# Two prompt steps of a head pair made one, and gate products in units of 512 and 256 tokens, in a one-core diffusion layer

## The chip, the cores and the metric

The kernel runs on one NeuronCore of a Trainium2 chip. Its engines run side by side and meet at semaphores: TensorE (PE, matmuls and transposes), VectorE (DVE), ScalarE (ACT), GpSimd (POOL), and SyncE (SP), which issues most DMAs. The metric is device time in microseconds (us); lower is better.

## The reference

One transformer layer serves 1024 latent tokens and 256 prompt tokens with the same weights. `D_IN` holds queries, keys and values of two attention branches, a gate `z` for each, and two merge gates.

```python
h = _rmsnorm(x) * (1.0 + scale) + shift
qa, ka, va, za, qb, kb, vb, zb, ga, gb = split(h @ w_in)
oa = attention_a(qa, ka, va)      # 8 heads; latent: 2-D neighbourhood + 512 cached keys, one softmax
ob = attention_b(qb, kb, vb)      # 8 heads on 2 kv heads, rotary, +-128 window + 512 cached keys + a sink logit
ya = (oa * silu(za)) @ w_br_a
yb = (ob * silu(zb)) @ w_br_b
y  = rmsnorm(x + gate * ((sigmoid(ga) * ya + sigmoid(gb) * yb) @ w_out))
```

Prompt tokens see only the 256 prompt tokens (branch b adds the sink logit there too). All is float32 in and out; each product is made of three passes of split operands.

## The kernel before

`front` makes the normalised, split input `h` ("hm") and the values. `pairs` then runs a loop over four pairs of heads for branch a and again for branch b (the last pair of b is written out apart), and `finish` does the two branch projections, the merge and the output.

A pair begins with projections (`project`: 6 for branch a, 3 for branch b, a third of them 256 tokens wide, the rest 512), each handled by ACT and DVE (`projected`; in branch b with the rotary arithmetic on DVE). Then come `STEPS` = 10 attention steps. Steps 0 and 1 are the prompt of head 0 and of head 1; steps 2 to 9 are blocks of latent queries (sample steps). Each step has 2 columns of softmax statistics (`t`). A step is a chain over four engines:

- PE `scores(s)` into PSUM `s_ps`; DVE `minima(s)` (scores are negated, so the maximum is a minimum; sample steps in branch a first add a bias that POOL prepares in `comb`); ACT `exps(s)`; DVE `normalise(s)`;
- PE `transposes(s, c)` in chunks `c` (two of four blocks, then one of four and one of two; a prompt step has one chunk) into two banks `t_ps`; ACT `high` and DVE `low` copy each chunk out in two parts;
- PE `weighted(s, 0)` and `weighted(s, 1)` (values times probabilities; a prompt step has only the first); ACT `low_half`, DVE `add_halves`.

The order on each engine is written by hand. On PE, step `s` is: `scores(s)`, `weighted(s-2, 1)`, the first two chunks of `transposes(s-1)`, `unit(s)`, the remaining chunks of `transposes(s-1)`, `weighted(s-1, 0)`. A `unit` is a piece of the gate products (3 blocks of 1280 tokens a pair, 24 matmuls per piece into the one PSUM bank `d_ps`). It is what PE does while the softmax chain of the step runs on DVE and ACT. There are 12 units of 320 tokens: one in each step, then `unit(10)` and `unit(11)` in the tail. ACT copies a unit to `gst` (two slots, a tile of its own) and stores it to DRAM (`gate`, `gate_out`).

In branch b, `scores(0)` stands ahead of the last projection (`EARLY` = 2) and the rest of the prompt chain is woven into it. In branch a it stands behind all projections.

SP loads in order: the caches of a pair into `craw` (after the previous pair's caches are split), a weight tile, the values `vw` and `vp`, bias blocks for `comb`, more weight tiles. Tiles are split on ACT and DVE (`tile_high`, `tile_low`) at the steps that the table `SPLITS` names.

Of the kernel before, what the change touches and what calls it, by code (L numbers as in the profile page):

```python
# [41 lines left out]
P = 128  # L42
# [25 lines left out]
UNIT = 320  # L68
UNITS = TOK // UNIT
# [3 lines left out]
STEPS = 10  # L73
CHUNKS = [1, 1] + [4] * 8
# [565 lines left out]
def pairs(nc, io, block, hm, ident, wt, wraw, craw, w_in, w_hi, w_lo, tiles, own, counts, earlier_stage, branch, f=None):  # L640
# [12 lines left out]
    q1, q2, kk, kc, pr, pt, ost, gst, otmp = (tiles[n] for n in ("q1", "q2", "kk", "kc", "pr", "pt", "ost", "gst", "otmp"))  # L653
# [8 lines left out]
    if A:  # L662
        comb, rowm, colm = (own[n] for n in ("comb", "rowm", "colm"))
        kout = otmp
# [12 lines left out]
    LAST_AT = 8  # L677
# [6 lines left out]
    EARLY = None if A else 2  # L684
    PROMPT_READY = 4 if A else 1
    COMB_FREE = [0, 0, 6, 10, 12, 14]
# [57 lines left out]
    def chunk_blocks(s):  # L744

        if s < 2:
            return [[(0, 0), (0, 1), (1, 0), (1, 1)]]
# [15 lines left out]
    def _(sp):  # L763
# [6 lines left out]
        def body(p, last):  # L770
# [16 lines left out]
            def load_caches():  # L787
                sp.wait_ge(c_split, pb * 3)
# [21 lines left out]
            sp.wait_ge(pvb_done, pb * (STEPS - 2))  # L810
# [62 lines left out]
    def _(pe):  # L873
        def body(p, last):
# [17 lines left out]
            def unit(u):  # L892

                i, t0 = PROJ + u // UNITS, (u % UNITS) * UNIT
                if u % UNITS == 0:
# [3 lines left out]
                pe.wait_ge(g_done, pb * GPP * UNITS + u)  # L899
                mm = split_mm(pe, d_ps[:, 0:UNIT], lambda a, k: tile(i, a, k),  # L900
                              lambda b, k: hm[:, b, k, t0:t0 + UNIT], KD)
                mm.then_inc(d_done, 1)

            def score(s, t, out, rhs):

                if s < 2:
                    h, cols = s, lambda ap: ap[..., LAT + t * P:LAT + (t + 1) * P]
                elif A:
                    h, cols = (s - 2) // 4, lambda ap: ap[..., (4 * t + (s - 2) % 4) * P:(4 * t + (s - 2) % 4 + 1) * P]
                else:  # L910
                    h, cols = t, lambda ap: ap[..., (s - 2) * P:(s - 1) * P]
# [3 lines left out]
            def scores(s):  # L915
# [6 lines left out]
                else:  # L922
                    if s == 2:
# [3 lines left out]
                for t in range(2):  # L927
                    if s < 2:
                        mm = score(s, t, s_ps[:, 2 * t, 0:PROMPT], lambda h, r: kk[r, h, LAT:TOK])
# [1041 lines left out]
```

## Time and profile before

| | us |
|---|---|
| median of 3 runs | 1283.93 (1282.22 to 1284.35) |
| the profiled execution's own time | 1281.49 |
| its span, first to last instruction | 1279.7 |
| PE busy | 1224.1 (96%) |
| DVE / ACT busy | 833.5 (65%) / 617.8 (48%) |
| granted TensorE clock | 0.993 of full speed |

A busy PE is not PE at its peak: ends of matmuls are modelled and overlap, so the length of a piece of work is read from its start to the start of the next.

### The profile page before, as it was taken

How to read it: one execution, taken by the hardware profiler on the slowest of the kernel's cores; microseconds unless marked ns; L12 is line 12 of the kernel's file. 1: busy time of each engine (PE TensorE's matmuls, PEld its weight loads, DVE VectorE, ACT ScalarE, POOL GpSimd, SP SyncE). 2: the span in 40 equal slices, each digit the busy share in tenths (PEclk: the TensorE clock that was granted, in tenths of full speed). 3: DMA queues.
4: the chain of work that ended last, by engine and by line, in shares of the span. 5: the costliest groups of instructions: out<-in, count | busy, mean ns of one | idle time of the engine just before them, and what ended most of it. 6: DMA issues, size and time to landing. Idle time of an engine off the chain costs nothing. (4 is left out here: it accounts for less than half of the span.)

```text
span 1279.7 us, 23385 instructions
## 1 busy us (share of the span) xinstructions
PE 1224.1 (96%) x7888; PEld 1111.7 (87%) x7888; DVE 833.5 (65%) x1674; ACT 617.8 (48%) x1239; POOL 194.7 (15%) x203
## 2 busy tenths in 40 slices
PE   6999999999999999999999989999999989899997
PEld 1599889988998899899889989989988988898996
DVE  2469458757755875687688588588678875444342
ACT  3432335534643554355466456546546664543441
POOL 0000023104300520231000000000000024433440
PEclk9999999999999999999999999999999999899999
DMA  9356532133214213321511411421221557444440
GB/s 360 134 182 193 195 115 75 55 122 118 74 59 139 79 62 110 123 67 52 181 55 38 132 48 37 116 65 37 74 90 39 189 170 241 149 148 148 159 154 33
DMA packets 87257, 147.67 MB, mean 115 GB/s; under 512 B 7558, under 2 KB 65542, under 8 KB 87180
## 3 DMA queue, kind: packets, MB, share of 16 engines
q1 hardware_dynamic: 70476, 124.64, 30.3%
q10 hardware_dynamic: 16704, 22.15, 4.8%
q8 instruction: 30, 0.49, 0.2%
q14 instruction: 47, 0.39, 0.1%
HBM read 111.37 MB, written 35.40 MB: 115 GB/s over the span
## 5 line engine op out<-in xcount | busy, mean ns | idle before, releaser
L83 PE MATMUL d_ps_pairs<-h,wt 128*128 128x320 f32 x2304 | 359.3, 311 | 0.0
L83 PEld LDWEIGHTS d_ps_pairs<-h,wt 128*128 128x128 f32 x2304 | 338.8, 188 | 0.3
L1087 ACT ACTIVATE pr<-s_ps_pairs,mx 128x896 f32<-128x896 f32 (+1 forms) x160 | 143.1, 897 | 84.4 <-DVE mx L1315 44.0
L1272 DVE TENSOR_TENSOR pt<-t_ps_pairs,pt 128x512 fp32r<-128x512 f32 (+1 forms) x272 | 158.3, 621 | 37.1 <-ACT pt L1076 35.8
L83 PE MATMUL s_ps_pairs<-h,wt 128*128 128x512 f32 (+1 forms) x864 | 167.6, 354 | 0.0
L83 PEld LDWEIGHTS s_ps_pairs<-h,wt 128*128 128x128 f32 x864 | 141.9, 189 | 21.9
L1076 ACT ACTIVATE pt<-t_ps_pairs 128x512 fp32r<-128x512 f32 (+1 forms) x272 | 135.1, 547 | 34.7 <-PE t_ps_pairs L949 29.1
L949 PE MATMUL t_ps_pairs<-ident_sb,pr 128*128 128x128 f32 x960 | 133.0, 276 | 13.0 <-DVE pt L1272 6.1
L949 PEld LDWEIGHTS t_ps_pairs<-ident_sb,pr 128*128 128x128 f32 x960 | 108.3, 140 | 23.2 <-DVE pt L1272 12.8
L1699 PE MATMUL y_ps<-wo,mg 128*128 128x512 f32 x480 | 113.2, 396 | 0.0
L1663 POOL TENSOR_TENSOR tp<-tp 128x256 f32<-128x256 f32 x40 | 31.3, 783 | 517.5 <-DVE tp L1751 516.2
L1699 PEld LDWEIGHTS y_ps<-wo,mg 128*128 128x128 f32 x480 | 90.0, 188 | 21.6
L864 POOL TENSOR_TENSOR comb_a<-rowm_a,comb_a 128x384 f32<-128x384 f32 x48 | 51.4, 1071 | 324.5 <-DMA comb_a<-in_bias 324.5
L1284 DVE TENSOR_REDUCE mn<-s_ps_pairs 128x2 f32<-128x1024 f32 (+1 forms) x72 | 83.6, 1162 | 23.9 <-PE s_ps_pairs L913 22.7
L1331 DVE TENSOR_SCALAR pr<-pr,rden 128x896 f32<-128x896 f32 (+1 forms) x160 | 96.2, 644 | 2.8
L83 PE MATMUL b_ps<-og,wb 128*128 128x256 f32 x720 | 90.0, 287 | 5.4 <-DVE tp L1751 5.4
L83 PEld LDWEIGHTS b_ps<-og,wb 128*128 128x128 f32 x720 | 89.0, 193 | 6.1 <-DVE tp L1751 4.0
L1136 ACT ACTIVATE otmp<-o_ps_pairs 64x256 f32<-64x256 f32 x80 | 30.5, 382 | 114.1 <-PE o_ps_pairs L977 113.3
L1104 ACT ACTIVATE gst<-d_ps_pairs 128x320 f32<-128x320 f32 x96 | 41.8, 435 | 79.5 <-PE d_ps_pairs L83 79.5
L83 PE MATMUL v_ps<-wv,h 128*128 128x320 f32 x480 | 73.1, 311 | 0.0
L83 PEld LDWEIGHTS v_ps<-wv,h 128*128 128x128 f32 x480 | 70.7, 188 | 1.0 <-issue 0.9
L1751 DVE TENSOR_TENSOR tp<-b_ps,gt 128x256 f32<-128x256 f32 x80 | 32.5, 422 | 44.1 <-PE b_ps L83 42.5
(168 smaller groups left out, 1687.4 us busy)
## 6 DMA issues: line engine op xcount, KB each, us to landing
gates_d<-gst ACTq DMA_DIRECT2D x96, 160.0 KB, 1.8
wraw<-in_w_gate SPq DMA_DIRECT2D x24, 512.0 KB, 3.5
gt<-gates_d SPq DMA_DIRECT2D x40, 256.0 KB, 4.0
comb_a<-in_bias SPq DMA_DIRECT2D x24, 384.0 KB, 3.4
vw_a<-v_d SPq DMA_DIRECT2D x64, 128.0 KB
v_d<-vst SPq DMA_DIRECT2D x20, 320.0 KB, 4.5
wada<-in_w_ada SPq DMA_DIRECT2D x12, 512.0 KB, 5.7
kk<-kb_d SPq DMA_DIRECT2D x16, 320.0 KB, 5.8
```

Of the source, the lines that this page charges most:

```text
L83: mm = eng.matmul(out, lhs(a, k), rhs(b, k), start=(k == 0 and i == 0), stop=(k == n_k - 1 and i == 2))
L864: pool.tensor_tensor(c, rm, c, ALU.subtract).then_inc(comb_t, 1)
L949: mm = pe.transpose(t_ps[:, n % 2, b * P:(b + 1) * P], probs_block(s, t, kb), ident[:, :])
L1076: act.activation(pt[:, 0, c * 512:c * 512 + cols], t_ps[:, n % 2, 0:cols], ACT.Copy).then_inc(hi_done, 1)
L1087: act.activation(probs_run(s, t), scores_run(s, t), ACT.Exp, bias=mx[:, t:t + 1], scale=-1.0, accum_out=den[:, t:t + 1]).then_inc(exp_done, 1)
L1104: act.activation(gst[:, u % 2, :], d_ps[:, 0:UNIT], ACT.Copy).then_inc(g_done, 1)
L1272: dve.tensor_tensor(pt[:, 1, c * 512:c * 512 + cols], t_ps[:, n % 2, 0:cols], pt[:, 0, c * 512:c * 512 + cols].bitcast(F32), ALU.subtract) ...
L1284: red = dve.tensor_reduce(ctx_min[:, :], s_ps[:, :, :].rearrange("p (t b) c -> p t b c", b=2)[:, :, s % 2 if s >= 2 else 0, 0:width], AX.X ...
L1331: dve.tensor_scalar(probs_run(s, t), probs_run(s, t), rden[:, t:t + 1], None, ALU.mult).then_inc(p_done, 1)
L1663: pool.tensor_tensor(tp[:, j % 2, 0, :], tp[:, j % 2, 0, :], tp[:, j % 2, 1, :], ALU.add).then_inc(summed, 1)
L1699: mm = pe.matmul(y_ps[:, e, n * 512:(n + 1) * 512], mg[:, a, k, e * P:(e + 1) * P], wo[k][:, b, n * 512:(n + 1) * 512], start=(k == 0 and ...
L1751: dve.tensor_tensor(tp[:, j % 2, br, :], b_ps[:, j % 2, br, 0:CT], gt[(j + 2) % GSLOTS][:, br, :], ALU.mult).then_inc(b_prod, 1)
```

## The change

Steps 0 and 1 become one step 0 with four columns (two heads by two blocks of queries), so `STEPS` = 9 and the sample steps are 1 to 8. Its scores fill four halves of two PSUM banks, its maxima, sums and reciprocals are four wide, and its eight transposed blocks are two full chunks. In branch a `scores(0)` and the maxima now also stand ahead of the last projection (`EARLY` = 5). In both branches all of `normalise(0)` comes behind it. The 12 units become 10, of 512 or 256 tokens, so there is one unit a step and one in the tail (`unit(9)`). The copies of the units go to `craw`, the buffer that the caches are loaded into, so the next pair's cache loads wait until all gate stores of this pair have landed, and the first copy of a pair waits until the caches are split. In `finish` the raw weights rotate over the staging buffers in another order, and the load into `craw` stands behind the last gate store.

```diff
-UNIT = 320
-UNITS = TOK // UNIT
+UNITS = [(0, 0, 512), (0, 512, 512), (0, 1024, 256), (1, 0, 512), (1, 512, 512), (1, 1024, 256),
+         (2, 0, 256), (2, 256, 256), (2, 512, 512), (2, 1024, 256)]
+NU = len(UNITS)
-STEPS = 10
-CHUNKS = [1, 1] + [4] * 8
+STEPS = 9
+SAMPLES = STEPS - 1
+CHUNKS = [2] + [4] * SAMPLES
...
+    gst = craw[:, :].rearrange("p (u c) -> p u c", u=2)
-        SPLITS = [(3, 0, 1), (4, 0, 2), (2, 1, 6), (0, 1, 9), (1, 1, STEPS)]
+        SPLITS = [(3, 0, 1), (4, 0, 2), (2, 1, 4), (0, 1, 7), (1, 1, STEPS)]
-        SPLITS = [(2, 0, 1), (0, 1, 2), (3, 0, 5), (1, 1, STEPS)]
+        SPLITS = [(2, 0, 1), (0, 1, 2), (3, 0, 4), (1, 1, STEPS)]
-    EARLY = None if A else 2
+    EARLY = 5 if A else 2
...
             def load_caches():
-                sp.wait_ge(c_split, pb * 3)
+                for slot in range(2):
+                    sp.wait_ge(g_out[slot], pb * (NU // 2) * 16)
...
             def scores(s):
-                    if s == 2:
+                    if s == 1:
                         pe.wait_ge(x_used, p * NG + NG)
                         pe.wait_ge(c_split, pb * 3 + 3)
...
-                    if s < 2:
-                        mm = score(s, t, s_ps[:, 2 * t, 0:PROMPT], lambda h, r: kk[r, h, LAT:TOK])
+                    if s == 0:
+                        for head in range(2):
+                            mm = score(s, t, prompt_scores(t, head), lambda h, r: kk[r, h, LAT:TOK], head)
                         continue
...
-                if 4 <= s < STEPS:
+                if 3 <= s < STEPS:
                     weighted(s - 2, 1)
...
-            unit(STEPS + 1)
             weighted(STEPS - 1, 1)
...
             def gate(u):
-                act.wait_ge(g_out[u % 2], (pb * (GPP * UNITS // 2) + u // 2) * 16)
-                act.activation(gst[:, u % 2, :], d_ps[:, 0:UNIT], ACT.Copy).then_inc(g_done, 1)
+                if u == 0:
+                    act.wait_ge(c_split, pb * 3 + 3)
+                act.wait_ge(g_out[u % 2], (pb * (NU // 2) + u // 2) * 16)
+                act.activation(gst[:, u % 2, 0:n], d_ps[:, 0:n], ACT.Copy).then_inc(g_done, 1)
...
-            gate(STEPS + 1)
-            gate_out(STEPS + 1)
+            gate_out(STEPS)
...
+            def prompt_minima():
+
+                dve.wait_ge(s_done, pb * STEPS + 1)
+                both = s_ps[:, :, :].rearrange("p (t b) (h c) -> p t b h c", b=2, h=2)[:, :, 0, :, :]
+                grid4 = lambda ap: ap[:, :].rearrange("p (t h) -> p t h", h=2)
                 if A:
+                    dve.tensor_reduce(grid4(mx), both, AX.X, ALU.min).then_inc(m_done, 2)
                     return
...
-                    if n == EARLY:
-                        normalise(0)
...
                 if n == EARLY:
-                    minima(0)
+                    prompt_minima()
                 projected(n)
+            normalise(0)
...
-        sp.wait_ge(c_split, 3 * ALL)
+        sp.wait_ge(s_done, ALL * STEPS)
         load_w(2)
-        sp.wait_ge(s_done, ALL * STEPS)
         load_w(3)
+        sp.wait_ge(w_lo, TILES_TOTAL)
         load_w(4)
...
+        sp.wait_ge(g_out[0], ALL * HALF * 16)
+        sp.wait_ge(g_out[1], ALL * HALF * 16)
+        load_w(5)
...
-        own_f.update(wb=wb, wo=wo, stage=[craw[:, :], x[:, 0, :], x[:, 1, :], wraw[:, :]])
+        own_f.update(wb=wb, wo=wo, stage=[x[:, 0, :], x[:, 1, :], wraw[:, :], craw[:, :]])
```

PE at the prompt of a branch a pair, before, from the last projection to the first sample scores (`h,wt` into `s_ps` is a projection, into `d_ps` a unit, `kk,q` are scores over own keys, `kc,q` over cached keys, `vp_a` the prompt's weighted sum):

```order
L83 MATMUL s_ps_pairs<-h,wt 128x512 x24
L912 MATMUL s_ps_pairs<-kk,q 128x256
...
L83 MATMUL d_ps_pairs<-h,wt 128x320 x24
...
L912 MATMUL s_ps_pairs<-kk,q 128x256
...
L949 MATMUL t_ps_pairs<-ident_sb,pr 128x128 x4
...
L83 MATMUL d_ps_pairs<-h,wt 128x320 x24
...
L977 MATMUL o_ps_pairs<-pt,vp_a 128x256 x4
...
L912 MATMUL s_ps_pairs<-kc,q 128x512
```

The same place of the change:

```order
L928 MATMUL s_ps_pairs<-kk,q 128x256
L929 MATMUL s_ps_pairs<-kk,q 128x256
...
L86 MATMUL s_ps_pairs<-h,wt 128x512 x24
...
L86 MATMUL d_ps_pairs<-h,wt 128x512 x24
...
L928 MATMUL s_ps_pairs<-kc,q 128x512
...
L966 MATMUL t_ps_pairs<-ident_sb,pr 128x128 x8
...
L86 MATMUL d_ps_pairs<-h,wt 128x512 x24
...
L995 MATMUL o_ps_pairs<-pt,vp_a 128x256 x8
```

All prompt scores moved ahead of the last projection. The first sample scores (`kc,q`) stand behind one unit of 512, where two units of 320 and two sets of prompt scores stood.

PE in the tail of a branch a pair, before:

```order
L83 MATMUL d_ps_pairs<-h,wt 128x320 x24
...
L949 MATMUL t_ps_pairs<-ident_sb,pr 128x128 x2
...
L977 MATMUL o_ps_pairs<-pt,vc_a 128x256 x8
...
L83 MATMUL d_ps_pairs<-h,wt 128x320 x24
...
L977 MATMUL o_ps_pairs<-pt,vw_a 128x128 x2
L977 MATMUL o_ps_pairs<-pt,vw_a 128x256 x4
L977 MATMUL o_ps_pairs<-pt,vw_a 128x128 x2
```

The tail of the change:

```order
L86 MATMUL d_ps_pairs<-h,wt 128x256 x24
...
L966 MATMUL t_ps_pairs<-ident_sb,pr 128x128 x2
L978 REGISTER_ALU
L995 MATMUL o_ps_pairs<-pt,vc_a 128x256 x8
L976 REGISTER_ALU
L995 MATMUL o_ps_pairs<-pt,vw_a 128x128 x2
L995 MATMUL o_ps_pairs<-pt,vw_a 128x256 x4
L995 MATMUL o_ps_pairs<-pt,vw_a 128x128 x2
```

The unit between the last two weighted sums (`vc_a`, then `vw_a`) is gone, so nothing stands between them now.

## Rows read from the trace of the kernel before

**Rows 1.** Busy time by stretch: one pair of branch a, one of branch b

```profile
core 0: us, PE busy (x) PEld busy (x) DVE busy (x) ACT busy (x) POOL busy (x), PEclk, DMA share, GB/s
380.60:497.60 117.00, 114.79 (x763) 107.35 (x762) 79.86 (x154) 56.83 (x114) 25.26 (x24) 1.00 0.28 91
720.00:825.00 105.00, 100.45 (x676) 94.06 (x675) 78.72 (x182) 57.91 (x133) 0.00 (x0) 1.00 0.23 68
```

**Rows 2.** Timeline of PE, a steady step: start, us, engine, line, operation [wait]

```profile
441.05 0.82 PE L949 MATMUL t_ps_pairs<-ident_sb,pr 128*128 128x128 f32 x6
...
442.65 0.39 PE L912 MATMUL s_ps_pairs<-kc,q 128*128 128x512 f32 x1
...
444.29 1.03 PE L977 MATMUL o_ps_pairs<-pt,vw_a 128*128 128x128 f32 x8
...
445.97 3.76 PE L83 MATMUL d_ps_pairs<-h,wt 128*128 128x320 f32 x24
449.58 0.82 PE L949 MATMUL t_ps_pairs<-ident_sb,pr 128*128 128x128 f32 x6
```

**Rows 3.** Timeline of PE, branch a, prompt scores to fourth step

```profile
408.24 0.28 PE L912 MATMUL s_ps_pairs<-kk,q 128*128 128x256 f32 x1
...
424.55 0.73 PE L977 MATMUL o_ps_pairs<-pt,vp_a 128*128 128x256 f32 x4 [0.83 <-DVE pt L1272]
...
434.00 0.40 PE L912 MATMUL s_ps_pairs<-kc,q 128*128 128x512 f32 x1
```

**Rows 4.** Timeline of PE, tail of that pair to the next pair's first projection

```profile
488.84 1.03 PE L949 MATMUL t_ps_pairs<-ident_sb,pr 128*128 128x128 f32 x8
...
497.64 2.73 PE L83 MATMUL s_ps_pairs<-h,wt 128*128 128x512 f32 x11
```

**Rows 5.** Timeline of PE, branch b, first unit to the transposes of step 3

```profile
734.35 3.68 PE L83 MATMUL d_ps_pairs<-h,wt 128*128 128x320 f32 x24
...
764.34 1.03 PE L949 MATMUL t_ps_pairs<-ident_sb,pr 128*128 128x128 f32 x8
```

**Rows 6.** Timeline of PE, a projection of 512 tokens in branch b

```profile
728.88 5.63 PE L83 MATMUL s_ps_pairs<-h,wt 128*128 128x512 f32 x24
```

**Rows 7.** Chain that ended last: start us, us, what (192 matmuls of 256 columns)

```profile
1135.49 23.04 PE b_ps L83 x192
```

**Rows 8.** Timeline of DVE, branch a, step 3: first reduction, then low copies

```profile
428.26 1.22 DVE L1284 TENSOR_REDUCE mn<-s_ps_pairs 128x2 f32<-128x1024 f32 x1
...
431.43 1.29 DVE L1272 TENSOR_TENSOR pt<-t_ps_pairs,pt 128x512 fp32r<-128x512 f32 x2
```

**Rows 9.** Page, part 5: the exponentials (mean of one)

```profile
L1087 ACT ACTIVATE pr<-s_ps_pairs,mx 128x896 f32<-128x896 f32 (+1 forms) x160 | 143.1, 897 | 84.4 <-DVE mx L1315 44.0
```

**Rows 10.** Timeline of DVE, branch b: prompt minima, last queries of the last projection

```profile
734.99 0.69 DVE L1284 TENSOR_REDUCE mn<-s_ps_pairs 128x2 f32<-128x512 f32 x1
...
741.15 1.39 DVE L1263 TENSOR_TENSOR q<-rot_b,q 64x512 fp32r<-64x512 f32 x2
```

**Rows 11.** Timeline of DVE, branch b, a steady step: first reduction, last low copies

```profile
772.18 1.23 DVE L1284 TENSOR_REDUCE mn<-s_ps_pairs 128x2 f32<-128x1024 f32 x1 [0.85 <-PE s_ps_pairs L913]
...
779.11 1.01 DVE L1272 TENSOR_TENSOR pt<-t_ps_pairs,pt 128x512 fp32r<-128x512 f32 x2
```

**Rows 12.** Timeline of SP, branch a, the pair's first tile load

```profile
384.76 0.33 SPq L785 DMA_DIRECT2D wraw<-in_w_gate  x1
```

**Rows 13.** Timeline of POOL, last operation on the pair's first bias block: pair 1, pair 3

```profile
185.02 1.88 POOL L866 TENSOR_TENSOR comb_a<-comb_a,colm_a 128x384 f32<-128x384 f32 x1
...
418.80 1.02 POOL L866 TENSOR_TENSOR comb_a<-comb_a,colm_a 128x384 f32<-128x384 f32 x1
```

**Rows 14.** Page, part 6: DMA issues of the gate stores, the last figure us to landing

```profile
gates_d<-gst ACTq DMA_DIRECT2D x96, 160.0 KB, 1.8
```

**Rows 15.** Source line 789, the cache key loads: time to landing

```profile
DMA to landing us min/median/max: 3.8/5.1/9.0
```

**Rows 16.** Timeline of PE, tail of the last pair and the first branch products

```profile
1025.80 1.03 PE L949 MATMUL t_ps_pairs<-ident_sb,pr 128*128 128x128 f32 x8
...
1037.12 4.58 PE L83 MATMUL b_ps<-og,wt 128*128 128x256 f32 x36 [1.28 <-DVE og L1452]
```

More of the change, by code:

```diff
@@ L744, in chunk_blocks @@
     def chunk_blocks(s):
-        if s < 2:
-            return [[(0, 0), (0, 1), (1, 0), (1, 1)]]
+        if s == 0 and A:
+            return [[(2 * h + kb, t) for kb in range(2) for t in range(2)] for h in range(2)]
+        if s == 0:
+            return [[(2 * h + kb, t) for h in range(2) for t in range(2)] for kb in range(2)]
         if A:
@@ L977, in weighted @@
                         mm = pe.matmul(o_ps[:, c0 * P:(c0 + nb) * P], v, pt[:, part, b0 * P:(b0 + nb) * P],
-                                       start=(half == 0 and n == 0 and part == 0),
-                                       stop=((half == 1 or s < 2) and n == len(work) - 1 and part == 1),
+                                       start=(half == 0 and part == 0 and (n == 0 or (s == 0 and c0 > 0 and n == 2))),
+                                       stop=(part == 1 and ((half == 1 and n == len(work) - 1)
+                                                            or (s == 0 and n % 2 == 1))),
                                        skip_group_check=True)
@@ L989, in body @@
             for s in range(STEPS + 1):
-                if s < STEPS and not (s == 0 and EARLY):
+                if 0 < s < STEPS:
                     scores(s)
-                if 4 <= s < STEPS:
+                if 3 <= s < STEPS:
                     weighted(s - 2, 1)
@@ L1086, in exps @@
                         act.wait_ge(r_done, pb * STEPS + s)
+                    if s == 0:
+                        for h in range(2):
+                            c = 2 * t + h
+                            ex = act.activation(prompt_probs(t, h), prompt_scores(t, h), ACT.Exp, bias=mx[:, c:c + 1],
+                                                scale=-1.0, accum_out=den[:, c:c + 1])
+                            if h == 1:
+                                ex.then_inc(exp_done, 1)
+                            if not A:
+                                es = act.activation(esk[:, c:c + 1], nsk[:, h:h + 1], ACT.Exp, bias=mx[:, c:c + 1],
+                                                    scale=-1.0)
+                                if h == 1:
+                                    es.then_inc(esk_done, 1)
+                        continue
                     act.activation(probs_run(s, t), scores_run(s, t), ACT.Exp, bias=mx[:, t:t + 1], scale=-1.0,
@@ L1140, in body @@
                     split_caches()
+                if A and n == EARLY:
+                    exps(0)
                 projected(n)
@@ L1151, in body @@
                     high(s - 1, range(min(2, CHUNKS[s - 1])))
-                if s < STEPS and not (s == 0 and EARLY):
+                if 0 < s < STEPS:
                     exps(s)
+                if s < STEPS:
                     gate(s)
@@ L1160, in body @@
                     tile_highs(s)
-                if last and s == 6:
-                    act.wait_ge(o_done, pb * STEPS + 4)
+                if last and s == 5:
+                    act.wait_ge(o_done, pb * STEPS + 3)
                     act.dma_start(io["o_d"][pb, :, 0:2 * P], ost[:, 0:2 * P]).then_inc(o_out, 16)
@@ new lines, in minima @@
+                if not A:
+                    dve.wait_ge(band_in, 16)
+                for t in range(2):
+                    near = comb[:, n % 2, t, :] if A else band[:, 0 if s == 1 else 2 if s == STEPS - 1 else 1, :]
+                    bank = near_bank(s, t)
+                    red = dve.tensor_tensor_reduce(bank, bank, near, 1.0, BIG, ALU.add, ALU.min, nm[:, t:t + 1])
+                red.then_inc(m2_done, 1)
+                dve.wait_ge(m1_done, p * SAMPLES + s if A else p * STEPS + s + 1)
@@ L1383, in body @@
                         first_gated(dve, f, 0)
-                if s < STEPS and not (s == 0 and EARLY):
+                if 0 < s < STEPS:
                     normalise(s)
```

194 lines of the change are left out of this document (94 added, 100 removed).

## The prediction

> **What bounds the kernel.** I read the busy time by stretch first. In one pair of branch a PE is busy 114.8 of 117.0 us, in one of branch b 100.5 of 105.0, at a granted clock of 1.00 [rows 1]; DVE, the next engine, has 79 us of work in either. So PE sets the pace, and there are two things to gain: the price of PE's own work, and the places where PE waits. The timeline of PE says where those are. A steady step of branch a has a period of 8.53 us: 1.60 for six transposes and the cached part of the weighted sum, 1.64 for scores, 1.68 for the near part and eight transposes (0.1 each), 3.61 for the unit, with no wait [rows 2]. The waits stand at both ends of a pair.
>
> Branch a, from the prompt scores to the scores of step 4, takes 25.76 us [rows 3]. The work in it is 0.96 of prompt scores (8 of 256 columns at 0.120 [rows 7]), 3.52 + 3 x 3.61 of units, 1.5 of transposes, 1.60, 3.28 of sample scores, 0.96 of prompt weighted sums: 22.65. So 3.1 us are lost; the longest single wait is 0.83, for DVE's low copies [rows 3]. The tail takes 8.80 us [rows 4] for 1.68 + 1.60 + 3.52 + 0.87 = 7.67 of work: 1.1 lost. In branch b, the 29.99 us from unit(0) to the transposes of step 3 [rows 5] hold 14.35 of units, 0.48 + 4.92 of scores, 3.1 of transposes and cached sum, 0.96 and 0.72 of weighted sums, 24.5 in all: 5.5 lost. A prompt step has little PE work of its own, and its chain is longer than one unit.
>
> **The change part by part, per pair.**
>
> *Units.* 320 tokens cost 24 x 147 ns = 3.52 us. 512 tokens with the same operand `h` cost 734.35 - 728.88 = 5.47 [rows 5, 6], 256 cost 24 x 0.120 = 2.88 [rows 7]. Twelve units are 42.24, five of each new size 41.75, and one change-over of 0.09 (3.61 against 3.52) goes: 0.6 us gained. That is about 11 ns a matmul beyond the columns, and 48 matmuls fewer.
>
> [...]
>
> *Step 1 (first sample step).* In branch a, `scores(0)` is followed by a projection and unit(0), 5.47 us each, so the prompt chain is covered. The next scores end 0.96 + 5.47 + 1.64 = 8.1 us after the projections, at 416.3 on the old scale. The old place of the first sample scores' end was 419.6. DVE first wants the bias block there, and POOL has it at 418.80 + 1.02 = 419.8 [rows 13]: 3.5 us late. But SP's work comes earlier. Its first tile load stood 4.1 us after the pair's start [rows 12, 1], because `tile_high` stood behind the copy and store of unit(11). Now the last unit ends some 5 us before the pair does, and the tile is split about 1.7 us sooner; the value loads and bias loads behind it on SP follow. So DVE is 1.8 late. Cover: from the scores' end PE has 0.8 of transposes, 5.47 of unit(1), 0.96 of weighted sum, 7.2 in all. The chain is 1.8 + 2.5 (minima: DVE's first copy stands 3.17 after its first reduction [rows 8], of which 2.5 is the minima) + 2 x 0.9 and read-outs of exponentials, some 2.1 [rows 9]: 6.4. Hidden, with 0.8 to spare. In the first pair the block comes at 186.9 [rows 13] in a pair begun at 145.7, 5.5 after it is wanted, with no tail ahead of it: PE waits 2.9 for the low copies and some 0.5 in the next step.
>
> *Step 2* has a unit of 256, and two `add_halves` ahead of the low copies. DVE begins 0.35 late (tile split of step 1), the low copies end 431.43 + 1.29 - 428.26 = 4.45 later [rows 8], plus 0.4 for the second addition. PE wants the first of two banks at 0.8 + 2.9 = 3.7 and gets it at about 4.5, the second later still: 1.0 us lost. This is the new place of the old wait.
>
> *Steps 5 to 7* also have 256. PE's period falls to 8.53 - 0.64 = 7.9 in branch a, 7.7 in b. DVE's chain in b is 779.11 + 1.01 - 772.18 = 7.94 from the scores to the last low copy [rows 11]; PE wants this at 7.7. I take 0.2 a step, 0.6. Branch a has no sink arithmetic and I take 0.
>
> *Branch b, step 1.* The sample scores need all queries, so they wait for the rotary work of the last projection. The old minima began at 734.99, the last query was done at 741.15 + 1.39 = 742.5 [rows 10], with 1.05 of `normalise(0)` in between, which now comes after. The minima are 0.45 longer. That makes 742.0. Unit(0) now ends at 734.35 + 0.48 + 5.47 = 740.3: PE waits 1.75. What is late next, `normalise(0)` (1.6 us), then lies beside the scores (1.64).
>
> *Tail.* The 1.1 lost there stays. unit(11) hid the last low copies; without it the near sum follows the cached sum (1.03) at once and waits 0.3.
>
> *craw.* The last gate store is issued some 3.9 us after the last unit and takes 1.8 to land [rows 14]; the caches follow, 5.1 at the median [rows 15], and are in 5.9 us into the next pair. ACT reaches them at 5.1 in branch b, where DVE takes them at 7.3 behind the first queries; 0.6 for ACT's first copy leaves about 1 us. Cost 0; this cover is thin.
>
> *Sums.* Branch a: before 3.1 + 1.1 = 4.2 lost. After: 0.2 (restarts) + 1.0 + 1.1 + 0.4 = 2.7. With 0.6 of units: 2.1 a pair, 6.3 for three; the first pair gives 2.1 + 1.1 (its own old wait was that much longer) - 3.4 = -0.2. Branch b: 6.6 before; after 1.85 + 1.0 + 0.2 + 0.6 + 1.4 = 5.05; with 0.6, 2.15 a pair, 6.5 for three. The last pair differs: from the end of its second last unit to 1037.12 takes 11.3 us, and the last wait is for DVE's `first_gated` chain [rows 16], which starts from the transposes and not from unit(11). Dropping unit(11) there saves nothing, while its tokens are done earlier: 41.75 - 11 x 3.52 = +3.0, less 2.2 of waits saved: 0.8 slower. In `finish` the new order of loads puts each ahead of its use, since its chain hangs on DVE and on stores of `o_d` after the same point: 0.
>
> Total -0.2 + 6.3 + 6.5 - 0.8 = 11.8, say 12 us, from the profiled span 1279.7 and the 1.8 around it: 1269.5. That execution was 2.4 below the median of the runs shown, so the median goes from 1283.9 to **1272**.
>
> **The rivals.**
>
> *Larger gain, 0.10.* DVE's order in step 2 leaves no wait, because the chunks arrive as in the old steady step, and the projection and unit prices hold. 8 x 1.0 more: 1264. Against it: 4.45 of chain on a cover of 3.7.
>
> *Bias late, 0.10.* SP's loads do not come sooner, since cache loads now stand in front of the tile. The chain in step 1 is then 8.1 against 7.2 and drags step 2: 1.4 for each of three pairs, 1276.
>
> *Short units expose the chain, 0.10, no change.* Each 256 step gives back the 0.64 by which its unit is shorter, wherever it stands: four steps a pair, 2.6 instead of the 1.0 to 1.6 taken, and the copies of 512 columns on ACT delay the transposes' copies by some 0.2 a step. 1.5 a pair, twelve in all: 1284. For it: DVE's 7.94 in branch b. Against: DVE waits 0.85 in that step [rows 11].
>
> *Caches late, slower, 0.10.* The loads wait for a store's landing and were early before. Branch b has four pairs with 1 us of slack; every further us comes off unit(0)'s cover and lengthens the wait at the first sample scores. The decisive point is a landing 3 to 4 us later than I take it, near the 9.0 maximum [rows 15]: beyond 10.5 us into the pair the 12 us are gone. At 12 us: 1288.
>
> [...]
>
> **How the numbers follow.** A measurement of this kernel tells about 0.2% (2.6 us) from no change. My forecast has 0.60 with its own range 1267 to 1277, from 1 us either way for step 2 over half the pairs, 0.5 for the wait of branch b at the first sample scores, and 0 to 0.5 for the tail. With the larger gain and the late bias that is 0.80 of faster, 0.10 of same and 0.10 of slower. The range for 8 in 10 reaches to both of the faster rivals: 1263 to 1280.
>
> **What would show it.** In the changed profile: unit steps of 5.5 and 2.9 us; a wait of PE on DVE's low copies behind the unit of step 2, near 1 us; in branch b a wait ahead of the first `kc,q` scores of 1.5 to 2; no wait ahead of the prompt's weighted sum, except in the first pair (about 3); pairs of about 115 and 103 us, the last about 105. It would be wrong if the cache loads land later than 7 us into a pair, if POOL's first block delays every pair, or if a step with 256 takes longer than 8 us.

## The result, and the profile after

The changed kernel takes 1297.2 us (median of 4 runs, 1294.6 to 1298.4) against 1284.1 for the kernel before: a ratio of 1.010, with a 95% interval of 1.008 to 1.012. It is 1% slower. The forecast was 1272, range 1263 to 1280; it missed in sign. The profiled execution has a span of 1296.6 us against 1279.7.

I read the busy time by stretch first, with one stretch for each pair (boundaries are PE's first projection of a pair; the last pair's ends at the first product of `finish`). The row behind the dots is a stretch of `finish`. The columns are those of [rows 1].

```profile
145.62:265.93 120.31, 115.77 (x715) 103.12 (x713) 79.76 (x152) 57.08 (x113) 25.25 (x26) 0.99 0.28 90
265.93:381.87 115.94, 113.95 (x714) 102.03 (x714) 79.21 (x152) 56.04 (x111) 22.96 (x24) 1.00 0.29 92
381.87:498.07 116.20, 114.20 (x714) 102.00 (x714) 79.87 (x152) 55.81 (x111) 22.95 (x24) 1.00 0.28 91
498.07:616.92 118.85, 115.16 (x715) 103.47 (x714) 78.85 (x152) 55.82 (x111) 23.06 (x25) 0.99 0.35 109
616.92:723.49 106.57, 100.55 (x622) 89.53 (x622) 78.16 (x178) 57.41 (x129) 0.00 (x0) 0.98 0.24 75
723.49:832.70 109.21, 101.85 (x623) 90.67 (x622) 78.22 (x178) 57.21 (x129) 0.00 (x0) 0.97 0.22 66
832.70:941.75 109.05, 102.27 (x622) 91.03 (x621) 78.23 (x178) 57.22 (x129) 0.00 (x0) 0.97 0.21 66
941.75:1048.36 106.61, 100.58 (x622) 88.34 (x621) 82.65 (x186) 62.53 (x137) 0.00 (x0) 0.99 0.30 101
...
1051.85:1152.29 100.44, 95.16 (x565) 85.58 (x566) 54.54 (x83) 47.38 (x71) 41.96 (x40) 0.94 0.57 186
```

Against the same points of the kernel before (118.0, 116.9, 117.0, 117.7 in branch a, 104.8, 104.8, 104.7, 107.5 in branch b; for the last pair up to the second group of products in `finish`, 1037.12 [rows 16] and now 1051.85), the pairs are longer by 2.3, -1.0, -0.8, 1.2, 1.8, 4.4, 4.3 and 2.6 us, and what follows by 2.2: the 17 us of the two spans. Two pairs of branch a go as forecast in kind. Most of what the forecast missed lies at the ends of pairs ahead of branch b, at the start of branch b's pairs, and in the granted clock, which is now 0.97 to 0.99 in six pairs instead of 1.00. The waits of PE and of ACT, summed, name the two places:

```profile
PE t_ps_pairs L966 <- DVE pt L1304: 18.3, 17, 2.8
...
PE s_ps_pairs L928 <- DVE q L1295: 8.8, 4, 3.2
```

```profile
ACT craw L1135 <- DMA gates_d<-craw: 19.0, 4, 5.0
```

(total us, times, longest.) Before, PE's first row stood at 6.1 us in 13 times, and its trace had neither of the other two.

**The tail.** Timelines of ACT, then of SyncE, then of PE, at the end of the first pair of branch b:

```profile
711.67 0.34 ACTq L1127 DMA_DIRECT2D gates_d<-craw  x1
...
717.69 0.38 ACT L1135 ACTIVATE craw<-d_ps_pairs 128x256 f32<-128x256 f32 x1 [4.64 <-DMA gates_d<-craw]
...
718.36 1.08 ACT L1093 ACTIVATE pt<-t_ps_pairs 128x512 fp32r<-128x512 f32 x2 [0.28 <-ACT craw L1135]
```

```profile
708.97 2.76 SPq L822 DMA_DIRECT2D kk<-kb_d  x4
```

```profile
716.23 0.96 PE L995 MATMUL o_ps_pairs<-pt,vw_b 128*128 128x256 f32 x6
719.73 1.54 PE L966 MATMUL t_ps_pairs<-ident_sb,pr 128*128 128x128 f32 x6 [2.54 <-DVE pt L1304]
720.92 2.02 PE L995 MATMUL o_ps_pairs<-pt,vc_b 128*128 128x256 f32 x8
```

The copy of the last unit, `gate(9)`, needs slot 1 of the raw buffer, which unit 7's store must have left. That store is issued only inside `gate(8)`, at 711.67. SyncE had begun four key loads of 320 KB at 708.97, and the store lands 5.9 us after its issue, where the median before was 1.8 [rows 14]. ACT stands for 4.64 us. Some 2.6 of them it would have stood anyway, since PE ends the unit near 715.6; so the store had 3.9 us and came 2.0 late. The high copies are behind it, DVE's low copies behind those, and PE's transposes wait 2.54. This happens at the four pair ends ahead of a pair of branch b (2.3 to 2.8 us) and at no other. Before, the store that the copy at 711.67 needed went out just ahead of the key loads, landed in 1.8 us and had 5.05. The one that the last copy needed, at 711.82, was behind those loads too and took 4.5 us, but unit(11) left it 7.75; ACT's rows of that kernel, then SyncE's:

```profile
706.62 0.34 ACTq L1098 DMA_DIRECT2D gates_d<-gst  x1
...
711.67 0.44 ACT L1104 ACTIVATE gst<-d_ps_pairs 128x320 f32<-128x320 f32 x1 [3.67 <-PE d_ps_pairs L83]
711.82 0.34 ACTq L1098 DMA_DIRECT2D gates_d<-gst  x1
...
719.57 0.44 ACT L1104 ACTIVATE gst<-d_ps_pairs 128x320 f32<-128x320 f32 x1 [4.29 <-PE d_ps_pairs L83]
```

```profile
706.69 2.47 SPq L807 DMA_DIRECT2D kk<-kb_d  x4
```

**The clock.** Busy time by stretch at that tail and at the next pair's first sample scores; the column behind the engines is the granted clock:

```profile
716.00:718.00 2.00, 1.19 (x11) 0.98 (x9) 0.00 (x0) 0.31 (x1) 0.00 (x0) 1.00 0.33 76
718.00:720.00 2.00, 0.27 (x2) 0.27 (x2) 1.01 (x2) 1.54 (x4) 0.00 (x0) 0.84 0.35 131
720.00:722.00 2.00, 2.00 (x11) 2.00 (x11) 1.23 (x4) 0.91 (x3) 0.00 (x0) 0.50 0.00 0
722.00:724.00 2.00, 2.00 (x16) 2.00 (x16) 0.53 (x2) 1.33 (x2) 0.00 (x0) 0.81 0.72 281
744.00:746.00 2.00, 0.00 (x0) 0.00 (x0) 1.49 (x4) 1.78 (x4) 0.00 (x0) 1.00 0.00 0
746.00:748.00 2.00, 1.00 (x2) 0.83 (x3) 1.89 (x7) 0.00 (x0) 0.00 (x0) 0.67 0.00 0
748.00:750.00 2.00, 2.00 (x7) 1.79 (x6) 0.36 (x2) 0.00 (x0) 0.00 (x0) 0.50 0.00 0
```

At both places PE has stood for 2.5 to 3.2 us, and then runs at 0.50; the rows come to 3.4 us of it at each. The eight scores from 747.00 take 3.12 us, up to 750.12, instead of 1.73 at full clock (experiment 6).

**The start of branch b's pairs.** Timeline of ACT in the second pair of branch b, and PE's wait there:

```profile
724.84 0.34 ACTq L1216 DMA_DIRECT2D o_d<-ost  x1
728.36 0.38 ACT L1071 ACTIVATE rot_b<-s_ps_pairs 128x256 f32<-128x256 f32 x1 [4.29 <-issue]
...
733.11 0.42 ACT L1049 ACTIVATE vc_b<-craw 128x256 fp32r<-128x256 f32 x1 [2.15 <-issue]
```

```profile
747.00 0.79 PE L928 MATMUL s_ps_pairs<-kc,q 128*128 128x512 f32 x1 [3.15 <-DVE q L1295]
```

The forecast had 1.75 for this wait. It is 1.85 in the first pair and 1.42 in the last, but 3.15 and 2.38 in the two pairs that ACT enters by the loop's jump back. There ACT is idle for nothing the profile shows ("issue"), once ahead of its first copy and once, five activations on, ahead of the value cache's. Before, ACT copied 0.87 us behind its last store's issue, and had no such idle. Queue q14, of the kind that the page calls "instruction", moved six blocks of 8 KB in the 20 us from 720, against three before (whose they were, the profile doesn't say):

```profile
q14 instruction: 6, 0.05, 0.8%
```

### The profile page after: what moved, and what is told of

Its sections match the earlier page's. It is cut to its first block and busy times, and to the rows that moved or that the text cites. A ratio compares the mean times of both kernels' runs of the same rounds, so it can differ in the third digit from the quotient of the medians.

```text
span 1296.6 us, 22309 instructions
## 1 busy us (share of the span) xinstructions
PE 1231.4 (95%) x7488; PEld 1080.5 (83%) x7488; DVE 830.4 (64%) x1650; ACT 610.9 (47%) x1215; POOL 186.0 (14%) x203
## 5 line engine op out<-in xcount | busy, mean ns | idle before, releaser
L86 PE MATMUL d_ps_pairs<-h,wt 128*128 128x512 f32 (+1 forms) x1920 | 351.9, 339 | 0.0
L86 PEld LDWEIGHTS d_ps_pairs<-h,wt 128*128 128x128 f32 x1920 | 295.2, 189 | 36.0
L1117 ACT ACTIVATE pr<-s_ps_pairs,mx 128x896 f32<-128x896 f32 x128 | 128.1, 1004 | 64.7 <-DVE mx L1326 36.7
L1314 DVE TENSOR_REDUCE mn<-s_ps_pairs 128x2 f32<-128x1024 f32 x64 | 78.0, 1219 | 41.7 <-POOL comb_a L881 24.3
L879 POOL TENSOR_TENSOR comb_a<-rowm_a,comb_a 128x384 f32<-128x384 f32 x48 | 43.5, 905 | 334.9 <-DMA comb_a<-in_bias 334.9
L1368 DVE TENSOR_SCALAR pr<-pr,rden 128x896 f32<-128x896 f32 x128 | 87.1, 722 | 2.2
L1135 ACT ACTIVATE craw<-d_ps_pairs 128x512 f32<-128x512 f32 (+1 forms) x80 | 39.0, 488 | 96.9 <-PE d_ps_pairs L86 77.7
L1168 ACT ACTIVATE otmp<-o_ps_pairs 64x256 f32<-64x256 f32 (+1 forms) x72 | 29.1, 404 | 117.2 <-PE o_ps_pairs L995 116.8
```

The costliest lines, as they stand in the source:

```text
L86: mm = eng.matmul(out, lhs(a, k), rhs(b, k), start=(k == 0 and i == 0), stop=(k == n_k - 1 and i == 2))
L879: pool.tensor_tensor(c, rm, c, ALU.subtract).then_inc(comb_t, 1)
L1117: act.activation(probs_run(s, t), scores_run(s, t), ACT.Exp, bias=mx[:, t:t + 1], scale=-1.0, accum_out=den[:, t:t + 1]).then_inc(exp_done, 1)
L1135: act.activation(gst[:, u % 2, 0:n], d_ps[:, 0:n], ACT.Copy).then_inc(g_done, 1)
L1314: dve.tensor_reduce(mn[:, 0:2], s_ps[:, :, :].rearrange("p (t b) c -> p t b c", b=2)[:, :, s % 2, :], AX.X, ALU.min).then_inc(m1_done, 1)
L1368: dve.tensor_scalar(probs_run(s, t), probs_run(s, t), rden[:, t:t + 1], None, ALU.mult).then_inc(p_done, 1)
```

## Experiments

Ratios are to the kernel before, measured on the same chip with the kernels beside it, each with its 95% interval; times are medians. "Changed" is 1.0101, from the runs of the result; it was not measured again beside the experiments.

**1. `e1_store7_early`: the store of unit 7 issued at the end of step 7.**

```diff
-                if u > 0:
+                if u > 0 and u != NU - 2:
                     gate_out(u - 1)
...
                     tile_highs(s)
+                if s == NU - 3:
+                    gate_out(s)
```

> The changed kernel with one edit: ACT issues the store of unit 7 at the end of step 7 instead of inside the gate copy of unit 8, which came 2.7 us behind the start of the key loads. Theory T (the last unit waits for the slot of unit 7, whose store stands behind the key loads): the wait of 4.6 us of ACT before the last unit's copy goes, the waits of 2.3 to 2.8 us on PE at the four tails ahead of B pairs fall under 0.6, and with them the half clock of the next 3 to 4 us; four times (2.0 + 1.3 to 2.0), so 13 to 16 us sooner than the changed kernel: about 1283, level with before. Rival C (late caches through the raw buffer are the cost): PE's waits at the tails only move to the next pair's first scores, and the time stays within 4 us of 1297. Rival U (the merged step and the units themselves): 8 us sooner at most, 1289.

1286.1 us, 1.0027 (1.0014 to 1.0041): 9.5 us off. Timeline of ACT at the same tail; no wait for a store is left in the whole trace:

```profile
714.13 0.38 ACT L1135 ACTIVATE craw<-d_ps_pairs 128x256 f32<-128x256 f32 x1 [3.04 <-PE d_ps_pairs L86]
```

PE waits 0.48 there instead of 2.54. The gain is less than expected, because PE's waits for the queries in the next two pairs grew to 4.00 and 3.83.

**2. `e2_kk_after_store`: the key loads wait for unit 7's store.**

```diff
                 sp.wait_ge(exp_done, pb * 2 * STEPS)
+                sp.wait_ge(g_out[1], pb * (NU // 2) * 16 - 16)
                 for h in range(2):
```

(The same wait stands ahead of the cos and sin loads.)

> The changed kernel with one edit: SyncE issues the key loads of B (and the cos and sin loads ahead of the first) only when the store of unit 7 has landed. The store is issued where it was. Theory T says it is the traffic ahead of the store that makes it late: the store then lands 2 us after its issue, ACT's wait ahead of the last copy falls from 4.6 to under 1 us, PE's waits at the tails to about 0.3 as in the A pairs, and the time is 1283 to 1286, if the key loads (5 us later, needed some 18 us later) stay hidden. If it is the late issue and not the traffic, ACT's wait stays over 2.5 us and the time over 1291. Rival C expects the caches not sooner and 1297.

1286.5 us, 1.0027 (1.0011 to 1.0043). The store is issued as late as in the changed kernel, but the copy that needs its slot no longer waits for it:

```profile
708.71 0.34 ACTq L1129 DMA_DIRECT2D gates_d<-craw  x1
...
712.69 0.38 ACT L1137 ACTIVATE craw<-d_ps_pairs 128x256 f32<-128x256 f32 x1 [2.59 <-PE d_ps_pairs L86]
```

Either edit alone removes the same wait: it takes both the late issue and the loads ahead of it. The cost here is that the first pair's caches come later: ACT waits 4.19 us for them, and PE 3.76 for the queries.

**3. `e3_caches_early`: the key cache waits for slot 0 alone, the value cache of branch b goes to free columns.**

```diff
-                for slot in range(2):
-                    sp.wait_ge(g_out[slot], pb * (NU // 2) * 16)
+                sp.wait_ge(g_out[0], pb * (NU // 2) * 16)
                 sp.dma_start(craw[:, 0:PAST], io["ck" + branch][p]).then_inc(craw_in, 16)
+                if A:
+                    sp.wait_ge(g_out[1], pb * (NU // 2) * 16)
+                else:
+                    sp.wait_ge(g_out[1], pb * (NU // 2) * 16 - 48)
-                sp.dma_start(craw[:, PAST:PAST + 4 * CH * HD], io["cv" + branch][p]).then_inc(craw_in, 16)
+                sp.dma_start(craw[:, V0:V0 + 4 * CH * HD], io["cv" + branch][p]).then_inc(craw_in, 16)
```

> The changed kernel with one edit: the key cache is loaded when unit 8's store has landed (its half of the raw buffer), and in B the value cache goes to columns that the last three odd units do not use, so both loads of B are issued about 4 us sooner, before the pair ends. Rival C (late caches): PE's wait ahead of the first cache scores in B (1.9, 3.2, 2.4, 1.4 us) falls by 1 us or more in each pair, and the time by 5 to 8 us to about 1290. Theory T: the query chain on DVE ends that wait, not the caches; the wait falls by 0.5 at most a pair and the time stays at 1294 to 1298.

1294.1 us, 1.0086 (1.0061 to 1.0110), not told apart from 1.0101. The loads of branch b now stand at 719.12 and 719.85, 3.9 us ahead of the pair's start at 723.0, and PE's waits for the queries are 1.85, 2.33, 3.24 and 1.43, in sum what they were. Late caches are not the cause in the changed kernel, where they had landed 2.6 to 4.1 us into each pair of branch b. ACT's two idle stretches are still there, with the caches long in:

```profile
724.30 0.34 ACTq L1220 DMA_DIRECT2D o_d<-ost  x1
727.49 0.39 ACT L1075 ACTIVATE rot_b<-s_ps_pairs 128x256 f32<-128x256 f32 x1 [3.96 <-issue]
...
731.73 0.42 ACT L1053 ACTIVATE vc_b<-craw 128x256 fp32r<-128x256 f32 x1 [1.65 <-issue]
```

**4. `e4_merge_320`: the merged prompt step with twelve units of 320.**

```diff
-UNITS = [(0, 0, 512), (0, 512, 512), (0, 1024, 256), (1, 0, 512), (1, 512, 512), (1, 1024, 256),
-         (2, 0, 256), (2, 256, 256), (2, 512, 512), (2, 1024, 256)]
+UNITS = [(b, t0, 320) for b in range(3) for t0 in range(0, TOK, 320)]
...
                 else:
                     weighted(s - 2, 1)
+                    unit(STEPS + 1)
...
+            unit(STEPS + 2)
             weighted(STEPS - 1, 1)
```

(ACT's copies of the two extra units follow in the same order.)

> The merged prompt step alone: the changed kernel with its units put back to twelve of 320 tokens (nine in the steps, three in the tail), still stored through the raw buffer. Rival U (uneven units and a tail with one unit are the cost): the pairs lose the 1.0 us of step 2 and the DVE waits, but pay the unit price of 0.6 a pair, and the time is 1284 or less, near before. Theory T: the tail copies have three slots to wait for instead of one and the store of unit 7 is still issued behind the key loads, so ACT's wait at the tail stays 3 to 5 us, though part of it lies beside the tail's units: 1288 to 1297.

1306.6 us, 1.0181 (1.0154 to 1.0208), beyond what either theory had, and ACT waits for a store only once (3.9 us) and not at each tail, as Theory T had it. PE's waits, summed:

```profile
PE o_ps_pairs L994 <- DVE pt L1307: 22.7, 16, 5.8
PE s_ps_pairs L927 <- DVE q L1298: 17.7, 4, 5.2
```

The prompt's chain and the queries' chain have 3.52 us of unit for cover where 512 tokens give 5.47: in branch a PE now waits 2.8 to 5.8 us ahead of the prompt's weighted sum, and in branch b 3.8 to 5.2 for the queries. So the wide first units are not a cost but what makes the merged step bearable. The arrangement of three units at the tail is mine, and part of the 9 us may be its. ACT's two idle stretches are absent here: the code has changed, and its loop lies elsewhere.

**5. `e5_act_written_out`: experiment 1, with ACT's loop over the first three pairs of branch b written out.**

```diff
-        with eng.Fori(0, PAIRS if A else PAIRS - 1) as p:
-            body(p, False)
+        if written_out:
+            for p in range(PAIRS - 1):
+                body(p, False)
...
-        turns(act, body)
+        turns(act, body, not A)
```

> The kernel with the store of unit 7 early, and ACT's loop over the first three B pairs written out in the code, with no jump back. Its trace had ACT idle on nothing the profile shows (issue) for 4.3 us at the start of B pairs 2 and 3 and again 2.9 to 3.1 us ahead of the value cache's copy, while the instruction queue moved five blocks there against three in the kernel before; PE's wait for the queries was 4.0 and 3.8 us in those pairs, 2.1 in the first, 1.4 in the last. Theory I (fetching ACT's instructions at the jump back makes the chain late): those waits fall to 1.4 to 2.1, and the two pairs shrink by 2 us each and about 1 more for the clock: 1286 becomes 1280 to 1282. Rival Q (the chain on DVE alone is too long for the cover): the waits stay at 3 us or more and the time within 2 us of 1286.

1278.0 us, 0.9962 (0.9948 to 0.9977): 8 us off experiment 1, and 0.4% faster than the kernel before. The second and third pair of branch b fall from 108.5 and 108.7 to 102.9 each, and their waits for the queries to 1.78 and 1.77. Both idle stretches are gone. In the first pair the value cache lands late (7.2 us behind its issue); ACT waits 3.55 for it, and PE 2.95 for the queries.

**6. `e6_filler`: experiment 1, with eight matmuls ahead of the first sample scores in branch b.** Their product is thrown away.

```diff
+                if s == 1 and not A:
+                    for k in range(8):
+                        pe.matmul(t_ps[:, 0, :], tile(2, 0, k % KD), hm[:, 0, k % KD, 0:512], start=True, stop=True)
```

> The kernel with the store of unit 7 early, and in B eight matmuls of 512 columns ahead of the first scores of step 1, whose product (in the transposes' bank) is thrown away: 1.9 us of added work that lies in the wait for the queries of 2.1, 4.0, 3.8 and 1.4 us. Theory K (what the wait costs beyond its length is the half clock behind it): the granted clock stays at 1 after step 1 in the first and last pair, the scores there take 1.64 us instead of 3.1, and the time falls by 1.3 to 2 us in each pair whose wait gets short, 3 to 6 in all: 1280 to 1283. Rival: the clock falls whatever PE does there, and the filler only adds up to 0.5 us in the last pair: 1286 to 1288.

1281.0 us, 0.9985 (0.9968 to 1.0001): 5 us off experiment 1, though 1.9 us of work was added in each of four pairs; what it fills are waits of 2.12, 4.00, 3.83 and 1.42 us. The first pair of branch b, timeline of PE in experiment 1 and then here:

```profile
636.11 0.77 PE L928 MATMUL s_ps_pairs<-kc,q 128*128 128x512 f32 x1 [2.12 <-DVE q L1297]
...
639.24 1.21 PE L966 MATMUL t_ps_pairs<-ident_sb,pr 128*128 128x128 f32 x8
```

```profile
631.65 1.97 PE L1011 MATMUL t_ps_pairs<-h,wt 128*128 128x512 f32 x8
633.68 0.49 PE L928 MATMUL s_ps_pairs<-kc,q 128*128 128x512 f32 x1
...
635.41 1.04 PE L966 MATMUL t_ps_pairs<-ident_sb,pr 128*128 128x128 f32 x8
```

The same scores take 3.13 and 1.73 us. From 600 to 1080 us no 2 us stretch with a clock under 0.90 is left, where experiment 1 has sixteen. Even the pairs whose wait is only shortened (2.0 and 1.5 us left) stay at full clock. Six of the sixteen lie behind the last tail, where the clock fell in some kernels and not in others; that part is not the filler's doing as far as is shown.

**7. `e7_combined`: experiments 1 and 3, with ACT's and DVE's loops written out.** No new diff.

> The store of unit 7 early, the caches early (the edit that moved nothing on its own), and ACT's and DVE's loops over the first three B pairs written out. If instruction fetch is what made the caches' earlier load worthless, all of it together gives PE waits of 1.4 to 2.0 at step 1 of every B pair and 1278 to 1281, faster than both kernels. If not, the same as with ACT's loop written out alone.

1274.7 us, 0.9942 (0.9920 to 0.9965). Every middle pair is now alike; one of branch a and two of branch b, by stretch:

```profile
494.80:610.50 115.70, 113.96 (x715) 102.02 (x714) 79.23 (x152) 55.89 (x111) 22.81 (x25) 1.00 0.37 112
610.50:713.90 103.40, 99.90 (x624) 88.29 (x622) 78.05 (x178) 56.98 (x129) 0.00 (x0) 1.00 0.25 76
713.90:817.20 103.30, 99.79 (x622) 88.22 (x621) 78.03 (x178) 56.84 (x129) 0.00 (x0) 1.00 0.21 66
```

**8. `e8_before_written_out`: the kernel before, with the same two loops written out.**

> The kernel before the change with ACT's and DVE's loops over the first three B pairs written out; a control for the two runs in which that made the changed kernel 8 us and 12 us faster. Theory I says that the jump back cost the changed kernel and hardly the kernel before: its trace has no idle of ACT there that is put down to issue, ACT starts 0.9 us behind its last store, and three blocks on the instruction queue, so 0 to 1 us a pair for DVE's 1.5 us restart, 1281 to 1284. Rival: any kernel of this form gains 4 to 8 us by it, 1275 to 1279, and then the gain found belongs to the loop and not to what the change did to it.

1281.2 us, 0.9991 (0.9979 to 1.0004). No change that can be told: what writing the loops out gains is a cost that the change brought.

**9. `e9_after_written_out`: the changed kernel, with the two loops written out and the store as it was.**

> The changed kernel with ACT's and DVE's loops over the first three B pairs written out and nothing else; the store of unit 7 stays late. If the two causes add, it is as much slower than the combined kernel (1275) as the changed kernel is over the one with the early store (10 to 11 us): 1285 to 1287. If the tail wait had only hidden the other, it stays at 1290 or more; if the late store mattered only because ACT came late out of the jump, it falls to 1280 or less.

1287.1 us, 1.0037 (1.0019 to 1.0056), as adding the two causes gives. ACT's wait before the last copy is 4.8 to 5.5 us again, and PE's 2.54 at the end of branch a and 2.65, 2.31 and 1.96 at the first three tails in branch b.

**10. `e10_no_early_caches`: experiment 7 without the early caches.**

> The combined kernel without its early cache loads: store of unit 7 early, ACT's and DVE's loops written out. Rival C in its last form (late caches bind once the fetches are out of the way) expects PE's wait at step 1 of B pairs at 2.5 us or more instead of 1.6, and 1277 to 1280 against 1275. If the caches are free, 1274 to 1276, the wait at 1.6 to 1.8 except perhaps in the first B pair, where the wait was 2.95 us with late caches and 1.63 with early ones.

1275.4 us, 0.9938 (0.9920 to 0.9956), with waits for the queries of 1.63, 1.60, 1.60 and 1.43. The caches cost nothing here. Against experiment 5 only DVE's loop is written out as well; in the profiles nearly all of the difference lies in the first pair of branch b (107.0 and 103.4 us), where the value cache was late.

**11. `e11_combined_filler`: experiment 7 with six thrown-away matmuls at that place.**

> The combined kernel with six thrown-away matmuls of 512 columns (1.4 us) ahead of the first scores of step 1 in B, where PE waits 1.6, 1.6, 1.6 and 1.4 us. In the combined kernel the granted clock falls only once, at the last tail (1032 to 1036 us), so if the clock is all that a filler can give back, this gives 0 to 2 us: 1273 to 1275. A time above 1276 would say that the filler's own work comes on top.

1274.4 us, 0.9934 (0.9917 to 0.9951). The waits of 1.6 us are filled and the pairs stay at 103.3: with no half clock to avoid, a filler gives nothing.

**12. `e12_loop_moved`: experiment 1, with ACT's first pair of branch a written out ahead of its loop.** Branch b's loop is unchanged, and lies further on in ACT's program: by the trace 172 instructions, each loop counted once, where the text below has 81.

```diff
+        if first_out:
+            body(0, False)
-        with eng.Fori(0, PAIRS if A else PAIRS - 1) as p:
+        with eng.Fori(1 if first_out else 0, PAIRS if A else PAIRS - 1) as p:
             body(p, False)
```

> Experiment 1 with ACT's first pair of branch a written out ahead of its loop (the loop runs over the other three). Branch b's loop is the same code, only 81 instructions further on in ACT's program; in the kernel before it began 22 further on than in the changed one. Theory P (where the loop lies decides how many blocks its jump has to fetch): ACT's start behind the jump, 3.5 us, and the second gap of 2.9 us change by 1.5 us or more in at least one of the two, PE's waits for the queries in pairs 2 and 3 of branch b (4.0, 3.8) move with them, and the time leaves 1286 by 3 us or more, either way. Rival L (it is the loop's own code, not its place): start, gap and waits stay within 0.5 us of experiment 1 and the time within 2 us.

1286.4 us, 1.0032 (1.0020 to 1.0045). The place of the loop decides the gaps in branch b: with the same code ACT now starts 1.7 us behind its last store, waiting only for PE, the second gap of 3.1 is gone, the instruction queue moves three blocks, and the waits for the queries are 1.85 in each of the three pairs, which take 105.6, 105.5 and 105.5 us. Timeline of ACT in the second pair of branch b:

```profile
718.95 0.34 ACTq L1220 DMA_DIRECT2D o_d<-ost  x1
720.66 0.38 ACT L1073 ACTIVATE rot_b<-s_ps_pairs 128x256 f32<-128x256 f32 x1 [2.49 <-PE s_ps_pairs L86]
...
723.27 0.42 ACT L1051 ACTIVATE vc_b<-craw 128x256 fp32r<-128x256 f32 x1
```

But the time did not leave 1286, as Theory P had it. Branch a's last two pairs are 1.3 and 1.6 us longer than in experiment 1, which gives back part of the 6.4 us of branch b, and it fits the theory: branch a's loop has moved as well, and behind its two jumps back ACT now idles 5.5 and 4.9 us for "issue", each time with three blocks on q14, where experiment 1 has neither. Timeline of ACT in the third pair of branch a:

```profile
383.26 0.59 ACT L1062 ACTIVATE q<-s_ps_pairs 64x512 fp32r<-64x512 f32 x1 [5.16 <-PE s_ps_pairs L86]
389.32 0.59 ACT L1065 ACTIVATE q<-s_ps_pairs 64x512 fp32r<-64x512 f32 x1 [5.47 <-issue]
```

The profiled execution is the fastest of its six (1281.5, at a clock of 0.992, where the other five have 0.987 to 0.989), so the rest of the account can't be read from it.

## Why the prediction was wrong

**The tail: the step that failed in branch b.** "The 1.1 lost there stays", with 0.3 for the near sum. I had DVE's and PE's part of the tail and left ACT's out: the slot that `gate(9)` needs. In branch a's first three tails and the last of branch b it held (0.3 us). Ahead of each pair of branch b the slot is late: 10.1 us of waits and the clock behind them. Before, the store was issued 0.07 us ahead of the key loads; after, it is 2.7 us behind them. And with unit(11) gone PE is done with the last unit 3.9 us behind the issue of the store that its slot waits for, where the last copy came 7.75 behind its own. The unit that moved was weighed, the store that it carries was not. Worth 9.5 us (experiment 1), or 12 once ACT's jump is out of the way (10 against 9).

**Branch b's step 1: right where it applied, with a cost that was not in the sum.** 1.75 us was forecast, and 1.4 to 1.85 was measured wherever neither the jump nor a late cache held ACT up. Where ACT came out of a jump late, the two pairs were 3 us longer, half clock included (experiment 12 against 1). Writing the loop out makes each 5.6 shorter, 8 us in all (experiment 5); the other 2.6 a pair are for the most part half clock (3.4 us of it, so 1.7 lost), which came behind the 1.85 us of experiment 12 and not behind the 1.78 of experiment 5. The trace of before has no such idle of ACT, and writing out that kernel's loops gains nothing (experiment 8). Experiment 12 shows that it is not the code but the place where the change put it.

**The clock: absent from the sum.** Before, it was at 1.00 in every pair, and I priced each wait at its length. Behind a wait that lets the clock fall the next scores alone cost 1.4 us more. In the first pair it fell behind the wait of 2.82 (190.29 to 193.71, some 1.7 us lost): most of the 2.3 by which that pair is longer, for 0.2 forecast. In `finish` it is the whole 2.2 us: the same 36 matmuls take 6.95 us, where the kernel before had 4.58 from 1037.12 on [rows 16].

**The raw buffer at no cost: right in the changed kernel**, by experiments 3 and 10. The cover is as thin as the forecast had it: with the caches in at 7.1, 7.9 and 8.7 us of the first pair of branch b (experiments 1, 5 and 2) PE's wait there rose to 2.12, 2.95 and 3.76. The rival of late caches, which alone forecast a slower kernel, fell; slower came by another way.

**Units: right.** In the third pair of branch a the unit that starts at 410.50 gives way to the scores at 415.94, 5.44 us later, for 5.47. PE's busy time in a pair of branch a fell from 114.8 [rows 1] to 114.0 to 114.2, for a forecast of 0.6. No term hangs on the "11 ns beyond the columns": the prices before, 120 ns a matmul of 256 columns [rows 7], 147 of 320 (24 from 493.25 to 496.77) and 228 of 512 [rows 5, 6], lie on one line, of 0.42 ns a column and 12 ns a matmul, an estimate from these three.

**Step 1 and step 2: right in branch b, short in branch a.** The first pair's wait was forecast at 2.9 and is 2.82 (1.8 to 2.7 in the experiments, but for the fourth). The bias came 2.0 us late for 1.8 (DVE begins at 419.56, the scores end at 417.57), and PE did not wait in that step, so that rival fell too. Step 2 loses 1.00 in branch b for 1.0; in branch a 0.71, and then 0.84 in step 3, 1.5 in all for 1.0:

```profile
431.13 1.03 PE L966 MATMUL t_ps_pairs<-ident_sb,pr 128*128 128x128 f32 x6 [0.71 <-DVE pt L1304]
...
435.63 1.14 PE L995 MATMUL o_ps_pairs<-pt,vw_a 128*128 128x128 f32 x8 [0.84 <-DVE pt L1304]
```

**The last pair: mis-sized.** Forecast 0.8 slower, measured 2.6, also in experiment 10. The chain to the last wait is 11.3 us as forecast (1040.54 to 1051.85); the near sum's new wait of 1.56 us lies inside it and costs nothing by itself. Up to 1040.54 PE has 3.0 us more of work, as forecast, but its waits there went only from 3.7 to 3.3 us: of the 2.2 us of saved waits 0.3 came.

With both faults out (experiment 10, by stretch between the same points), the pairs gain 1.7 on average in branch a for 2.1, and 1.5 in branch b for 2.15; the first loses 2.0 for 0.2, the last 2.6 for 0.8. By its ratio that kernel is 8 us faster than the one before, for 12 forecast: the mechanism was there, a third smaller. But it needs two loops written out, which the change did not have.

## What to carry to other kernels

When a unit of work is moved or dropped, move its store and the slot behind it in the sum too: ask when the store is issued, what loads are in the queues by then, and which engine stands in line for the slot. Price a wait of a busy TensorE by its length only where the trace shows the clock staying up behind it; useless matmuls that fill it are a quick way to tell (experiment 6: 5 us less). If an engine is idle for "issue" only in the iterations that a jump back opens, write that loop out on that engine before looking for data that comes late (8 us in experiment 5): here an edit in branch a moved the loops of both branches, which took the idle of ACT out of branch b and brought 5.5 and 4.9 us of it into branch a (experiment 12).

## What was not expected of the hardware

- The granted clock was at 0.50 within or right behind every single wait of PE of 2.0 us or more in a pair but one (2.79 us, experiment 4), for 3.4 or 6.8 us. The same wait of 1.85 us had it in experiments 2, 3 and 12 and not in the changed kernel. It was never there behind the waits of 1.6 for the queries of branch b, but behind one of 1.56 at the last tail it was, for 10 us, in the changed kernel and experiments 1, 3, 5 and 9, and in experiment 8 once behind waits of 0.99 and 0.50. So the length of a wait alone does not settle it. Filling 1.9 us with useless matmuls in four pairs came with 5 us less.
- A 128 KB store landed 5.9 us after its issue behind 1.28 MB of loads, though another engine had issued it, in its own queue.
- ACT's start behind a loop's jump took 3.5 us in the changed kernel, 0.9 in the kernel before, and 1.7 with the loop further on (experiment 12), with six, three and three blocks of 8 KB on the instruction queue. Experiment 12 shows that the place decides, in branch b for the better and in branch a for the worse (5.5 and 4.9 us of "issue"). That ACT stands for its own instructions there is my reading; the traces show neither whose the blocks were nor what makes one place better than another.
